# Chunk inverses of an RWKV scan by 32-token blocks, and two of four modulation products moved behind them

## What is computed

```python
def rwkv_scan(decay, k, v, a_vec, b_vec, r, state0, reverse):
    '''RWKV-7 state recurrence S <- S (diag(w) + a^T b) + v^T k, read out y = S r.'''
    def step(S, inp):
        w_t, k_t, v_t, a_t, b_t = inp[:5]
        sa = jnp.einsum('bhij,bhj->bhi', S, a_t)
        S = S * w_t[:, :, None, :] + sa[..., None] * b_t[:, :, None, :] + v_t[..., None] * k_t[:, :, None, :]
        y = jnp.einsum('bhij,bhj->bhi', S, inp[5]) if emit else None
        return S, y
    S, ys = lax.scan(step, state0, xs, reverse=reverse)
    return S, (jnp.moveaxis(ys, 0, 1) if emit else None)
...
mod = cond @ ada_w[i] + ada_b[i]
```

## Time and profile before

| | |
|---|---|
| median of 3 runs | 4356.01 us (4354.9 to 4359.01) |
| profiled execution, its own time | 4348.76 us |
| its span | 4347.0 us |
| TensorE matmuls busy | 3510.7 us, 81% |
| TensorE weight loads busy | 1732.7 us, 40% |
| VectorE busy | 1175.8 us, 27% |
| ScalarE busy | 590.0 us, 14% |
| mean granted TensorE clock | 0.923 of full speed |

### The profile page before, as it was taken

The page is one execution under the profiler, slowest core; times in us unless marked ns, Lnnn a source line. Parts: engine busy times, 40 slices in busy tenths (PEclk is TensorE's granted clock), DMA queues, the critical chain, the costliest instruction groups (busy, mean ns, idle before and its releaser), DMA issues. The chain is left out here.

```text
span 4347.0 us, 51301 instructions
## 1 busy us (share of the span) xinstructions
PE 3510.7 (81%) x22536; PEld 1732.7 (40%) x22536; DVE 1175.8 (27%) x1971; ACT 590.0 (14%) x1116; POOL 6.5 (0%) x28
## 2 busy tenths in 40 slices
PE   3778898686897787777777769998899593889998
PEld 1446877432333422222222234444444243444443
DVE  0244565623101300000000012663466004122210
ACT  0122232011000100000000011232212002111100
POOL 0000000000000000000000000000000000000000
PEclk7889999797998699999999989999999796999999
DMA  9014224011112079999999911111333223312220
GB/s 322 29 54 157 81 93 146 4 51 40 58 58 78 1 294 421 421 417 422 421 420 421 420 35 61 58 40 39 90 129 131 61 79 97 116 58 78 77 72 35
DMA packets 220098, 661.68 MB, mean 152 GB/s; under 512 B 30624, under 2 KB 94820, under 8 KB 169189
## 3 DMA queue, kind: packets, MB, share of 16 engines
q1 hardware_dynamic: 218120, 657.85, 39.6%
q10 hardware_dynamic: 1757, 0.56, 0.1%
HBM read 635.70 MB, written 20.19 MB: 151 GB/s over the span
## 5 line engine op out<-in xcount | busy, mean ns | idle before, releaser
L2298 PE MATMUL banks<-h_T,weight_ring 128*128 128x512 f32 x1408 | 608.6, 593 | 3.7 <-PEq L89 3.7
L1729 PE MATMUL banks<-weight_ring,xe_T 128*64 128x512 f32 x2048 | 467.1, 598 | 148.9 <-DMA weight_ring<-in_exp_w 146.7
L2298 PEld LDWEIGHTS banks<-h_T,weight_ring 128*128 128x128 f32 x1408 | 265.9, 190 | 332.7 <-issue 332.6
L1549 PE MATMUL banks<-weight_ring,ffn_act 128*128 128x512 f32 x704 | 307.0, 599 | 51.7 <-PEq L2465 44.7
L1729 PEld LDWEIGHTS banks<-weight_ring,xe_T 128*64 128x64 f32 x2048 | 142.2, 136 | 463.2 <-issue 257.1
L1744 PE MATMUL banks<-weight_ring,hid_T 128*64 128x512 f32 x1024 | 235.5, 602 | 86.0 <-DMA weight_ring<-in_exp_w 85.1
L1549 PEld LDWEIGHTS banks<-weight_ring,ffn_act 128*128 128x128 f32 x704 | 135.3, 193 | 223.3 <-issue 223.3
L2357 DVE SCALAR_TENSOR_TENSOR conv<-banks,cols,conv 128x510 f32<-128x510 f32 (+1 forms) x176 | 131.8, 749 | 341.1 <-ACT conv L2327 336.4
L1798 DVE TENSOR_TENSOR hid<-silu,banks 128x1024 f32<-128x1024 f32 x16 | 19.5, 1221 | 660.2 <-issue 566.5
L546 PE MATMUL banks<-h_T,weight_ring 128*128 128x512 f32 x416 | 180.5, 592 | 3.2 <-PEq L89 3.2
L1744 PEld LDWEIGHTS banks<-weight_ring,hid_T 128*64 128x64 f32 x1024 | 71.2, 137 | 249.3 <-issue 141.9
(11 more groups left out here) (536 smaller groups left out, 3956.5 us busy)
## 6 DMA issues: line engine op xcount, KB each, us to landing
weight_ring<-in_exp_w SPq DMA_DIRECT2D x192, 2048.0 KB, 11.2
weight_ring<-in_ada_w SPq DMA_DIRECT2D x24, 2048.0 KB, 10.3
weight_ring<-in_ffn_w_up SPq DMA_DIRECT2D x44, 1024.0 KB, 6.6
weight_ring<-in_mod_w SPq DMA_DIRECT2D x12, 2048.0 KB, 8.8
weight_ring<-in_ffn_w_down SPq DMA_DIRECT2D x10, 2048.0 KB, 7.8
weight_ring<-in_attn_w_in SPq DMA_DIRECT2D x7, 2048.0 KB, 7.9
weight_ring<-in_w_in SPq DMA_DIRECT2D x6, 2048.0 KB, 10.2
weight_ring<-in_w_in SPq DMA_DIRECT2D x9, 1024.0 KB, 7.8
```

The costliest lines, as they stand in the source:

```text
L1549: mm = pe.matmul(k.ps[:, 2 * t + n, :], left(kt)[:, t * P:t * P + P], src[:, n * 512:n * 512 + 512], start=kt == 0, stop=kt == total - 1)
L1729: mm = pe.matmul(k.ps[64 * half:64 * half + 64, 2 * c + b % 2, :], xeT[:, kt, e * CAP:(e + 1) * CAP], w[:, r, 512 * b:512 * b + 512], star ...
L2298: mm = pe.matmul(k.ps[:, b + c, :], w[:, c, kt, m * P:m * P + P], hT[:, kt, :], start=kt == 0, stop=kt == 7)
```

## The change

The inverse is now built from blocks of 32 tokens. Each 64x64 block has two 32x32 diagonal blocks `h`; with the two heads that makes four 32x32 tiles on the diagonal of the array, written to partitions 64g+32h. `LEVELS` is 4; a fifth, joining level computes only the off-diagonal 32x32 block of each 64x64 one. `T` now holds both T (columns 0 to 255) and its transpose (256 to 511) in packed 32-column form, and ACT expands the transpose into `TT`, whose other parts POOL clears once. The first pairs come from new products of 32 columns (`corners`), so `LT` goes, and `NB` gets products of its own. The sigmoid of `a` has its own buffer `a`, since `TT` now has to keep its zeros. Of the four modulation products of a round two stay in front, and the third and fourth come after the second and the fourth level. Cut to its core:

```diff
-    LEVELS = 5
+    LEVELS = 4
+    MOD_BANK = (2, 5, 6, 7)
...
+            pool.memset(W["TT"][:], 0.0).then_inc(pool_done, 1)
...
+            def corners(n, d, bank):
+                for x, (left, right) in enumerate((("A", "B"), ("B", "A"))):
+                    for q, (j, c) in enumerate(tiles):
+                        for h in range(2):
+                            for g in range(2):
+                                at32 = slice(j * P + c * 64 + 32 * h, j * P + c * 64 + 32 * h + 32)
+                                mm = pe.matmul(k.ps[quarter(g, h), bank, 256 * x + 32 * q:256 * x + 32 * q + 32],
+                                               W[left][half(g), d, at32], W[right][half(g), d, at32], start=True, stop=True)
+                ev(("LL", n, d), mm)
...
+            def doubling(name, d, bank, left, right):
+                for q in range(8):
+                    for h in range(2):
+                        for g in range(2):
+                            mm = pe.matmul(k.ps[quarter(g, h), bank, 32 * q:32 * q + 32], left(d, g, h, q), right(d, g, h, q), start=True, stop=True)
+                ev(name, mm)
...
-                for m in range(4):
-                    k.ring.wait(pe, 4 * n + m)
-                    ev(("mod", 4 * n + m), M.products(pe, k, 4 * n + m, (6, 7, 2, 5)[m]))
+                for m in range(2):
+                    modulate(4 * n + m)
...
                     products(("L", n, d), n, d, 6 + d, "A", "B")
+                    corners(n, d, 4 * d)
-                    pairs(("LT", n, d), n, d, 4 * d, "B")
+                    if latent(n):
+                        products(("NB", n, d), n, d, 4 * d + 1, "B", "R")
...
-                        products(("Y", n, l, d), n, d, 3 * d, "L", "TT")
+                        doubling(("Y", n, l, d), d, 3 * d, L_, TT_)
...
-                        products(("X", n, l, d), n, d, 3 * d + 1, "T", "Y")
-                        if l < LEVELS - 1:
-                            products(("XT", n, l, d), n, d, 3 * d + 2, "Y", "T")
+                        doubling(("X", n, l, d), d, 3 * d + 1, T_, Y_)
+                        doubling(("XT", n, l, d), d, 3 * d + 2, Y_, T_)
+                    if l % 2:
+                        pe.wait_ge(act_done, act_n[("trA" if l > 1 else "trK", n, 1)])
+                        modulate(4 * n + 2 + l // 2)
...
+                    for q in range(8):
+                        for g in range(2):
+                            mm = pe.matmul(k.ps[quarter(g, d), 3 * d, 32 * q:32 * q + 32],
+                                           W["L"][quarter(g, 1 - d), d, q * 64 + 32 * d:q * 64 + 32 * d + 32], TT_(d, g, 1 - d, q),
+                                           start=True, stop=True)
+                    ev(("Y", n, LEVELS, d), mm)
...
+                    for g in range(2):
+                        for h in range(2):
+                            ins = act.activation(W["TT"][quarter(g, h), d, :].rearrange("p (q n) -> p q n", q=8)[:, :, 32 * h:32 * h + 32],
+                                                 eighth("T", d, 1)[quarter(g, h)], ACT.Copy)
+                    ev(("TT", n, d), ins)
...
-                        ev(("Y", n, l, d), dve.tensor_tensor(masks("Y", d), one(3 * d), bcast(k.half[:, sides[d]["level"] + l, :], 8), ALU.mult))
+                        ev(("Y", n, l, d), dve.tensor_tensor(eighth("Y", d, 0), small(3 * d), bcast(k.quarter[:, sides[d]["level"] + l, :], 8), ALU.mult))
```

More of the change, by code:

```diff
@@ L214 @@
 N_SQ = 4
-HALF = {n: i for i, n in enumerate(["eye", "lower", "upper", "lower_eq", "upper_eq", "pair_lower", "pair_upper"])}
-HALF_LEVEL, HALF_LEVEL_T, N_HALF = 7, 12, 17
+HALF = {n: i for i, n in enumerate(["eye", "lower", "upper", "lower_eq", "upper_eq"])}
+N_HALF = 5
+QUARTER_LEVEL, QUARTER_LEVEL_T, N_QUARTER = 4, 8, 12
 def rows(ap, k0, kt, c0, width):
@@ L287, in __init__ @@
         self.square = sb("square", [P, N_SQ, P])
-        self.half = sb("half_square", [P, N_HALF, 64])
+        self.half, self.quarter = sb("half_square", [P, N_HALF, 64]), sb("quarter_square", [P, N_QUARTER, 32])
         self.misc = sb("misc", [P, 16])
@@ L1038, in pairs, with modulate @@
                 ev(name, mm)
+            def corners(n, d, bank):
[7 more added lines that the diff above has]
+                ev(("LL", n, d), mm)
+            def modulate(m):
+                k.ring.wait(pe, m)
+                ev(("mod", m), M.products(pe, k, m, MOD_BANK[m % 4]))
+            def doubling(name, d, bank, left, right):
[4 more added lines that the diff above has]
+                ev(name, mm)
             def turn(name, d, bank, source):
@@ L1144, in copy, with modulated @@
                 ev(name, act.activation(to, k.ps[:, bank, :], ACT.Copy))
+            def modulated(m):
+                act.wait_ge(pe_done, pe_n[("mod", m)])
+                act.sem_inc(k.ring.used, 1)
+                if m > 1:
+                    act.wait_ge(spread_done[m % 2], 64 * (m // 2))
+                ev(("mod", m), act.activation(M.part[:, m % 2, :], k.ps[:, MOD_BANK[m % 4], :], ACT.Copy))
             for n in range(ROUNDS):
@@ L1173, in _ @@
                     for j in range(4):
-                        ins = act.activation(W["K"][:, d, j * P:j * P + P], W["TT"][:, d, j * P:j * P + P], ACT.Identity,
+                        ins = act.activation(W["K"][:, d, j * P:j * P + P], W["a"][:, d, j * P:j * P + P], ACT.Identity,
                                              scale=k.col("rw_k_a", j), bias=B.fac[:, 66 + j:67 + j])
                     ev(("km", n, d), ins)
-                for m in range(4 * n, 4 * n + 4):
-                    act.wait_ge(pe_done, pe_n[("mod", m)])
-                    act.sem_inc(k.ring.used, 1)
-                    if m > 1:
-                        act.wait_ge(spread_done[m % 2], 64 * (m // 2))
-                    ev(("mod", m), act.activation(M.part[:, m % 2, :], k.ps[:, (6, 7, 2, 5)[m % 4], :], ACT.Copy))
+                for m in range(2):
+                    modulated(4 * n + m)
                 for d in range(2):
@@ L1188, in _ @@
                     copy(("W", n, d), flat("W", d), d)
+                for m in (2, 3):
+                    modulated(4 * n + m)
+                if n == 0:
+                    act.wait_ge(pool_done, pool_n["blank"])
+                for d in range(2):
+                    act.wait_ge(dve_done, dve_n[("TTl", n, LEVELS - 1, d)])
+                    for g in range(2):
+                        for h in range(2):
+                            ins = act.activation(W["TT"][quarter(g, h), d, :].rearrange("p (q n) -> p q n", q=8)[:, :, 32 * h:32 * h + 32],
+                                                 eighth("T", d, 1)[quarter(g, h)], ACT.Copy)
+                    ev(("TT", n, d), ins)
+                for d in range(2):
+                    act.wait_ge(pe_done, pe_n[("X", n, LEVELS, d)])
+                    for g in range(2):
+                        ins = act.activation(W["TT"][quarter(g, d), d, :].rearrange("p (q n) -> p q n", q=8)[:, :, 32 - 32 * d:64 - 32 * d],
+                                             small(3 * d + 1)[quarter(g, d)], ACT.Copy)
+                    ev(("X", n, d), ins)
                 for d in range(2):
```

96 lines of the change are left out of this document (59 added, 37 removed).

## The result

| | before | changed |
|---|---|---|
| median | 4355.99 us | 4515.23 us (4504.2 to 4518.14, 4 runs) |
| profiled execution, its own time | 4348.76 us | 4515.43 us |
| TensorE's matmuls, weight loads busy | 3510.7, 1732.7 us | 3551.2, 1745.2 us |
| mean granted TensorE clock | 0.923 | 0.891 |

The changed kernel takes 1.036 times as long as the one before, 95% interval 1.0342 to 1.0378: slower, by 159 us in the median. The forecast was 4490, the range 4400 to 4555.

A forecast was written before the change was run, and what follows sets the result against it. The array paced the old doublings; instruction fetch, 3.5 us per 256 TensorE instructions, would bound the new. Four latent rounds at +23.1 us and two context at +21.3 gave +135: 4348.76 to 4484, median 4490, range 4400 to 4555.

The forecast's parts named there:

- The cycle of 3.5 us a block: In the scan, fetching 256 TensorE instructions takes 3.3 to 3.7 us without weight loads; this sets the pace, chance 0.82.
- Rival (a): Whole scan: instructions arrive in time, so the array and the chain between engines set the pace; -93 us, 4263; chance 0.10.
- Rival (b): Doublings and the part before: TensorE issues evenly at 14.8 ns an instruction, not fetch-bound; +92 us, 4448; chance 0.05.
- Rival (c): Whole kernel: gain and loss cancel, with a cycle near 2.0 us or more front gain; under 0.2% remains; chance 0.03.
- Part 1: Front of each round: two modulation products leave, A times B starts 3.5 us in instead of 13.84; -10.3 us.
- Part 2: From the first product of A and B to the doublings: 1408 instructions, not 896; 23.9 us against 18.80, +5.1.
- Part 3: Doublings, join and two modulation products: 13.25 blocks at 3.5 us, plus loads and ACT's copies; 51.9 against 26.58, +25.3.
- Part 4: From U to the next round's modulation: a delayed fetch, +1.5 us, and a possibly lower clock, +1.5; +3.0 a round.
- The forecast's 7 us: Whole kernel: the runs' median lies 7 us above the profiled execution, 4356.01 against 4348.76; used to reach the median forecast.

The follow-up runs named there:

- the padded kernel: The changed kernel with an extra 32-row, one-column matmul ahead of every second matmul of the doublings, 1536 instructions a round; 4652.32 us, ratio 1.0685.

## Why the prediction was right, step by step

*The sign and the mechanism.* Shown. The cycle of 3.5 us a block, read from the earlier trace rows, was 3.55 in the four windows of the changed kernel and 3.58 over eleven cycles of the run without products between; what was varied alone (the array's work, its clock, the count of instructions) moved the time only where it changed the count. What is not shown is why a cycle has the 1.1 us before its packet and the 1.4 us behind it.

Rival (a), instructions in time, would have needed levels of about 3.3 us; they took 8.2 to 11.7. Rival (b), an even pace of 14.8 ns an instruction, falls too: between two restarts 256 instructions keep TensorE busy for 1.30 us, 5.1 ns each, or 1.93 at the lower clock, and then it stands. Rival (c) asked for a cycle near 2.0 us, and the shortest quiet one was 3.33. The page of the Trainium skill that spoke for (a) (Runtime: NRT & Kernel Launch, Instruction fetch mechanics) has crossings of blocks mostly hidden. The traces do not agree, with 60 stops of up to 4.7 us in the doublings of one kernel.

The size came out through errors that partly cancel. Growth of the profiled scan over six rounds, in us (it begins 0.3 us earlier in the changed kernel):

| | forecast | measured |
|---|---|---|
| part 1, modulation in front | -61.8 | -57.0 |
| part 2, to the doublings | +27.0 | +42.6 |
| part 3, doublings and join | +151.8 | +157.3 |
| part 4, from U on | +18.0 | +11.7 |
| sum | +135.0 | +154.6 |

*Part 1, the modulation leaves the front.* 3.5 us forecast, 3.57 measured in rounds 3 to 5. But in rounds 0 to 2 the front took 6.7, 5.4 and 5.5 us, at a granted clock of 0.62 to 0.65, round 1 for instance:

```profile
427.61 5.46 PE L396 MATMUL banks<-weight_ring,silu_c 128*32 128x512 f32 x32
```

5.46 instead of 3.64 us. The forecast took round 4 for all six.

*Part 2, from there to the doublings.* This term was mis-sized most. 23.9 forecast, 25.46 measured in round 4, and 25.4 to 27.1 in all six rounds. The growth forecast was 5.1 us for a latent round and, with half a block less, 3.3 for a context round; it was 6.7 to 8.4 and 5.0 and 7.7. The sum had taken half of the fetches there as quiet cycles of 3.5. The run with the first pairs as before puts the growth down to the new products, corners and NB, since the stretch is then back at its old length; which of their cycles were longer than priced was not taken apart.

*Part 3, the doublings.* 51.9 forecast, 53.15 measured in round 4 and 52.9 in the mean (49.4 to 55.4). Its pieces were mis-sized one against the other, so that its total came out close partly by luck. Thirteen blocks were priced at 45.5 us and took 47.05 in the run with the products in front. The two modulation products with their loads and ACT's copies were priced at 4.8 + 0.9 + 0.7 = 6.4, and the two runs differ by 5.8 a round in the mean. Of these 5.8, 2.3 are U's wait for ACT, put at 0.7; 3.5 are left for the products and loads, put at 5.7. The 3.2 us that a load was priced at do not follow from its own cycles either: 5.1 to 6.5 instead of 3.5 are 1.6 to 3.0. U's wait in round 4:

```profile
830.95 1.97 PE L1041 MATMUL banks<-x 64*64 64x64 f32 x32 [2.12 <-ACT x L1261]
```

```profile
826.73 3.39 ACT L1255 ACTIVATE x<-x 32x256 f32<-32x256 f32 x8
830.14 1.55 ACT L1261 ACTIVATE x<-banks 32x256 f32<-32x256 f32 x4
```

I had priced the copies as two full ones at most. They are twelve for the two directions, each of 32 partitions and 256 elements, and they follow one another every 0.39 to 0.42 us where a full one of 128 by 512 takes 0.60: an eighth of the elements at two thirds of the price. They also stand behind ACT's copy of the fourth modulation product, which could not begin before that product's end at 826.01. With all four products in front U waited at most 0.2 us for ACT in a round, so it is this order, and not the copies alone, that costs the 2.3 us.

*Part 4, from U on.* +3.0 a round forecast; 24.06 - 22.85 = +1.2 measured in round 4, 1.2 to 2.5 in the six.

*The sum.* +23.1 forecast for a latent round, +24.2 in round 4, where part 2 and part 3 came out 1.6 and 1.3 too low and part 4 was put 1.8 too high. Over the six rounds the scan ends 154.3 us later (at 960.34 instead of 806.02) where 135 were forecast, 3.2 us a round. Four fifths of that are part 2, and the rest is part 1; the errors of parts 3 and 4 cancel, which nothing in the working had provided for.

*The rest.* 12 us of the profiled execution's 167 lie behind the scan, where nothing was changed. Ten of them are in one stretch, before and changed:

```profile
3640.00:3976.00 336.00, 281.75 (x1204) 144.29 (x1202) 85.32 (x127) 54.44 (x91) 0.00 (x0) 0.91 0.26 93
```

```profile
3796.60:4142.30 345.70, 290.12 (x1206) 149.06 (x1203) 85.34 (x127) 54.45 (x91) 0.00 (x0) 0.87 0.26 90
```

The same work at a granted clock of 0.87 instead of 0.91. In the profiled executions of the other kernels the same instructions took 335.7 to 344.5 us, short and long ones among those with 32-token blocks and those without, so it is not put down to the change. The forecast's 7 us from the profiled execution of before to the median covers more than half of the 12.

## What to carry to other kernels

Before cutting matmuls into smaller ones, count instructions as well as columns. Here 256 instructions of TensorE took a cycle of 3.3 to 4.3 us, without other DMA traffic, however little they gave the array to do, so the doublings, at 3.80 us per 256, had almost no room: half the columns in each product and nearly twice the instructions doubled their time. Compare the instruction queue's packets with the stops marked "issue" at every 256th instruction; where they meet, as here, fewer instructions helped, and more work for each of them cost nothing. And a wait for a weight ring can be moved alone: two products out of the front gave 0.8% with the blocks left as they were.

## What the runs showed of the hardware

- The next block of 256 instructions is asked for only about 1.1 us after TensorE has gone over into the last one fetched (restart 785.39, packet from 786.47), so in these traces the fetching does not run further ahead than that.
- Weight loads on the same DMA engines lengthen that cycle: 5.1 and 6.5 us in the earlier trace rows, up to 6.9 us in the padded kernel, and stops of 0.68 and 2.27 us between products of 64x64 tiles, where a kernel without such loads in that place had none.
- Alternating a 64x64 matmul with one of 64x1 cost 0.52 us a pair, where 16 matmuls of 64x64 alone come in 0.93 us. 32x1 matmuls between 32x32 ones were far cheaper but not free: 256 instructions of that mix, a third of them of the small kind, are 2.2 us of busy time at the lower clock, against 1.93 for 32x32 ones alone.
- With 64 columns moving in place of 32, the granted clock in the windows above was 1.00 instead of 0.50, and the mean over the kernel 0.913 instead of 0.891, at the same time per block. The 7 us by which that kernel's median lies under the changed one's fit this, but the intervals overlap.
- On ScalarE a copy of 32 by 256 elements took 0.42 us, one of 128 by 512 0.60. Four such copies, one for each quarter of the partitions, take 1.7 us for half the elements of the full one.
